# MoBA heads issued in pairs, and the in-projection of block 2 as rounded products of split operands

## What is computed

```
s_own = einsum('bhqd,bhkd->bhqk', q_c, k_own) + bias_own     # masked where key > query
probs = softmax(logits);  out = einsum('bhqk,bhkd->bhqd', p_own, v_own)
```

```
u = h @ w_in
u_q, u_k, u_v, u_cq, u_ckv, u_kr, pool_in = split(u)
```

## Time and profile before

| | us |
|---|---|
| median of 3 runs | 2493.61 |
| lowest and highest run | 2492.33, 2496.37 |
| the profiled execution, own time | 2489.61 |
| its span | 2487.5 |
| PE busy in the span | 2416.9 |
| DVE busy | 1606.2 |
| ACT busy | 1038.0 |

### The profile page before, as it was taken

The page is one execution under the profiler, slowest core; times in us unless marked ns, Lnnn a source line. Parts: engine busy times, 40 slices in busy tenths (PEclk is TensorE's granted clock), DMA queues, the critical chain, the costliest instruction groups (busy, mean ns, idle before and its releaser), DMA issues. The chain is left out here.

```text
span 2487.5 us, 41693 instructions
## 1 busy us (share of the span) xinstructions
PE 2416.9 (97%) x17447; PEld 2057.1 (83%) x17447; DVE 1606.2 (65%) x2242; ACT 1038.0 (42%) x1365; POOL 98.9 (4%) x179
## 2 busy tenths in 40 slices
PE   8999999999999999999999999889999998988999
PEld 7999989999999999899999844454888887647999
DVE  6887756778888887567788533662644443464555
ACT  5445534454454455344544322651422222263333
POOL 2010000001101100000010000000000000000000
PEclk9999999999999999999999999999999999999999
DMA  8776503648777775126477741102433231212452
GB/s 281 252 268 219 162 3 124 208 137 281 251 238 255 268 245 154 34 70 223 146 251 253 281 126 68 35 1 81 156 102 102 86 101 52 85 52 68 158 197 69
DMA packets 270807, 381.97 MB, mean 154 GB/s; under 512 B 9593, under 2 KB 235209, under 8 KB 268994
## 3 DMA queue, kind: packets, MB, share of 16 engines
q1 hardware_dynamic: 251628, 314.47, 38.7%
q0 software_dynamic: 18128, 64.20, 7.2%
q10 hardware_dynamic: 902, 1.15, 0.2%
HBM read 366.13 MB, written 13.65 MB: 153 GB/s over the span
## 5 line engine op out<-in xcount | busy, mean ns | idle before, releaser
L704 PE MATMUL ps<-span 128*128 128x512 f32 x1280 | 453.7, 398 | 1.4 <-issue 1.2
L635 PE MATMUL ps<-span,w_low 128*128 128x256 f32 x1440 | 408.4, 284 | 0.0
L706 PE MATMUL ps<-span,w_low 128*128 128x256 f32 x1280 | 359.4, 281 | 0.0
L633 PE MATMUL ps<-span 128*128 128x256 f32 x1216 | 348.9, 287 | 7.7 <-DVE span L1585 4.7
L1603 DVE TENSOR_TENSOR w_low<-ring,span 128x2048 fp32r<-128x2048 f32 x131 | 299.5, 2286 | 78.1 <-ACT span L1267 78.0
L1267 ACT ACTIVATE span<-ring 128x2048 fp32r<-128x2048 f32 x131 | 250.5, 1914 | 132.3 <-DMA ring<-in_ffn_w_in 110.1
L704 PEld LDWEIGHTS ps<-span 128*128 128x128 f32 x1280 | 240.6, 188 | 59.3 <-issue 1.3
L635 PEld LDWEIGHTS ps<-span,w_low 128*128 128x128 f32 x1440 | 277.2, 192 | 0.0
L634 PE MATMUL ps<-span 128*128 128x256 f32 x864 | 245.6, 284 | 0.0
L633 PEld LDWEIGHTS ps<-span 128*128 128x128 f32 x1216 | 234.1, 193 | 11.8 <-DVE w_low L1603 4.8
L706 PEld LDWEIGHTS ps<-span,w_low 128*128 128x128 f32 x1280 | 241.9, 189 | 0.0
(11 more groups left out here) (487 smaller groups left out, 5340.7 us busy)
## 6 DMA issues: line engine op xcount, KB each, us to landing
ring<-in_ffn_w_in SPq DMA_DIRECT2D x88, 1024.0 KB, 8.9
ring<-in_w_mlp SPq DMA_DIRECT2D x64, 1024.0 KB, 5.3
wmod<-in_w_mod POOLq DMA_DIRECT2D x96, 512.0 KB, 6.8
ring<-in_ffn_w_out SPq DMA_DIRECT2D x44, 1024.0 KB, 5.1
ring<-in_w_mix_in SPq DMA_DIRECT2D x26, 1024.0 KB, 5.6
ring<-in_xattn_w_kv SPq DMA_DIRECT2D x16, 1024.0 KB, 5.5
mod_scratch<-mod_acc POOLq DMA_DIRECT2D x24, 512.0 KB, 6.3
ring<-mod_scratch SPq DMA_DIRECT2D x12, 1024.0 KB, 5.0
```

Source lines behind the costliest of these rows:

```text
L633: mm(dst, w_hi, x_hi, start=start, stop=False, **more)
L635: return mm(dst, w_lo, x_hi, start=False, stop=stop, **more)
L704: mm(ps[bank + m].rearrange("p (w t) -> p w t", w=2), hi[:, k, cols], span[:, :, k, :], start=(k == 0), stop=False, skip_group_check=True)
L706: last = mm(ps[bank + m][:, 0:T], lo[:, k, cols], h_high[:, k, :], start=False, stop=(k == KD - 1), skip_group_check=True)
```

## The change

1. **MoBA in pairs.** PE's order becomes, for p = 0 to 5: scores(pair p), the transposes of both heads of pair p-1, out(pair p-2). Within a pair the bias products come first, then six score products of 128 columns that alternate between the two heads, and four value products that alternate likewise. Waits are taken once for the pair. DVE's and ACT's programs are not changed.
2. **In-projection split.** The input's high half goes to `in_high` (written by ACT's shift), its low half to `h_low`, made by DVE two at a time behind the scales of the next chunk. Each weight tile is rounded by ACT (`in_high_part`) and split by DVE (`in_low_part`), two tiles ahead. All products become `split_mm` with weights stationary; the values now come out by column and are transposed by four PE transposes inside the last tile, which also widens from 32 to 128 columns (its DMA from 128 KB to 512 KB). The order within the first tile becomes chunk by chunk for both halves.
3. **Moved.** The running sums for pooling move from `qm` to `vm`, the pooled result from `vm` to `qm`, since the new buffers lie over `qm`, `km`, `probT` and part of `prob`. The padding memsets move from the pooling stage into the loop over MLA query heads, cut by head. In layer 1 pooling is done for the latent stream alone. The copy of a gain at the start (L3274) goes. In layer 1 the first rounding waits for the wide MLP's last use of `prob` and stands ahead of the squares on ACT.

```diff
-            for h in range(NH + 3):
-                if h < NH:
-                    scores(h)
-                if 2 <= h < NH + 2:
-                    turn(h - 2)
-                if h >= 3:
-                    out(h - 3)
+            for pair in range(NPAIR + 2):
+                if pair < NPAIR:
+                    scores(pair)
+                if 1 <= pair <= NPAIR:
+                    turn(2 * pair - 2)
+                    turn(2 * pair - 1)
+                if pair >= 2:
+                    out(pair - 2)
...
+                early, late = slice(0, P), slice(P, T)
+                for at, q, key in ((0, late, slice(0, P)), (P, late, slice(P, T)), (T, early, slice(0, P))):
+                    for e, bank in enumerate(banks):
+                        hi = slice(e * HD, (e + 1) * HD)
+                        last = mm(bank[:, at:at + key.stop - key.start], mq[hi, pair, q], mk[hi, pair, key],
+                                  start=False, stop=(at == T), skip_group_check=True)
...
+            def out(pair):
+                pe.wait_ge(*pt_ready.at(l, 2 * pair + 2))
+                if pair >= 2:
+                    pe.wait_ge(*av_out.at(l, pair - 1))
+                for k in range(2):
+                    for e in range(2):
+                        h = 2 * pair + e
+                        dst = ps[6 + pair % 2][e * HD:(e + 1) * HD, k * P:T]
+                        last = mm(dst, mv[:, k, h * HD:(h + 1) * HD], probT[:, e, k * T:T + k * P],
+                                  start=(k == 0), stop=(k == 1), skip_group_check=True)
```

```diff
+                pe.wait_ge(*part_low.at(i, n + 1))
                 if n >= 2:
                     pe.wait_ge(*in_evac.at(i, 2 * (n - 1)))
...
+                def product(m, k, c):
+                    ms = slice(m * P, (m + 1) * P)
+                    x_hi = in_high[:, 1, k, :] if c.start else in_high[:, :, k, :]
+                    return split_mm(ps[bank + m][:, c], hi[:, k, ms], lo[:, k, ms], x_hi, h_low[:, k, c],
+                                    k == 0, k == KD - 1)
...
+                if n == 0:
+                    for k in range(KD):
+                        pe.wait_ge(*h_low_ready.at(i, 2 * k + 2))
+                        for m in range(2):
+                            last = product(m, k, ask)
...
+        def in_high_part(i, n):
+            s, use = place(("in", i, IN_TILES[n][0]))
+            act.wait_ge(w_loaded[s].sem, 16 * (use + 1))
+            size = KD * IN_TILES[n][2]
+            go(w_in_high[(n + 1) % 2][:, 0:size], ring[:, s, 0:size], ACT.Copy).then_inc(*part_rounded.up())
...
             else:
+                act.wait_ge(*wide_act.at(0, 3 * KD * WIDE_QUARTERS))
+                in_high_part(i, 0)
                 for q in range(4):
                     for s in (CTX, LAT):
                         square(i, 0, s, q)
...
                 act.wait_ge(w_used[s].sem, use + 1)
+                if n + 2 < len(IN_TILES):
+                    in_high_part(i, n + 2)
...
-            for k in range(KD):
+            in_low_part(i, 0)
+            for k in range(KD + 1):
                 for s in (CTX, LAT):
-                    scale(i, 0, s, k)
+                    if k < KD:
+                        scale(i, 0, s, k)
+                for s in (CTX, LAT):
+                    if k:
+                        low(i, 0, s, k - 1)
+            in_low_part(i, 1)
...
                 roped(slice(0, MQK), ps[2 + u % 2][0:MQK, 0:T], qm[0:MQK, u, cols(LAT)])
+                for padded in (qm, km):
+                    step(i, v.memset(padded[MQK:P, u, :], 0.0), pool_dve)
```

More of the change, by code:

```diff
@@ L786, in moba, with scores @@
         def moba(l):
[L787 to L800, removed]
+            def scores(pair):
+                if pair >= 2:
+                    pe.wait_ge(*sm_act.at(l, 4 * (pair - 1)))
+                banks = [ps[SCORE_BANKS[(2 * pair + e) % 4]] for e in range(2)]
+                for e, bank in enumerate(banks):
+                    h = 2 * pair + e
+                    mm(bank[:, 0:T], cst["flip"], hank[:, h, :], start=True, stop=False,
+                       skip_group_check=True)
+                    mm(bank[:, T:T + P], cst["flip"], hank[:, h, P:T], start=False, stop=False,
+                       skip_group_check=True)
+                early, late = slice(0, P), slice(P, T)
+                for at, q, key in ((0, late, slice(0, P)), (P, late, slice(P, T)), (T, early, slice(0, P))):
+                    for e, bank in enumerate(banks):
+                        hi = slice(e * HD, (e + 1) * HD)
+                        last = mm(bank[:, at:at + key.stop - key.start], mq[hi, pair, q], mk[hi, pair, key],
+                                  start=False, stop=(at == T), skip_group_check=True)
+                        if at == T:
+                            last.then_inc(*sc_done.up())
             def turn(h):
@@ L809, in turn @@
                 last.then_inc(*pt_done.up())
[L811 to L814, removed]
+            def out(pair):
+                pe.wait_ge(*pt_ready.at(l, 2 * pair + 2))
+                if pair >= 2:
                     pe.wait_ge(*av_out.at(l, pair - 1))
[L816 to L820, removed]
+                for k in range(2):
+                    for e in range(2):
+                        h = 2 * pair + e
+                        dst = ps[6 + pair % 2][e * HD:(e + 1) * HD, k * P:T]
+                        last = mm(dst, mv[:, k, h * HD:(h + 1) * HD], probT[:, e, k * T:T + k * P],
+                                  start=(k == 0), stop=(k == 1), skip_group_check=True)
+                        if k:
+                            last.then_inc(*av_done.up())
             pe.wait_ge(*mix_evac.at(l, MIX_TILES - 1))
@@ L2267, in build_second @@
         mod_high = [mod_three[:, j * PIECE:(j + 1) * PIECE] for j in range(3)] + [mod_fourth]
+    with ExitStack() as under:
+        part = lambda name, shape: under.enter_context(nc.sbuf_tensor(name, shape, F32R))
+        part("below_in", [P, BELOW_IN])
+        w_in_high = [part("w_in_high0", [P, SLOT])[:, :]]
+        in_high = part("in_high", [P, 2, KD, T])
+        part("below_prob", [P, BELOW_PROB])
+        w_in_high.append(part("w_in_high1", [P, SLOT])[:, :])
     h_high = [h_both[:, s] for s in range(2)]
@@ L3270, in vector_program @@
         for i in range(DEPTH):
-            v.tensor_copy(key_gain[0:NOPE, i:i + 1], pcol(i, "g_k_mla", rows=NOPE)).then_inc(*key_gain_ready.up())
-        dve.wait_ge(*key_gain_ready.now(0))
-        for i in range(DEPTH):
             ub, ask = unit_base(i), asked(i)
@@ L3287, in vector_program @@
             for m in range(2):
-                for s in range(2):
-                    g = 2 * m + s
-                    step(i, v.tensor_tensor_scan(csum[:, g, first:first + T], ones_row, pin[:, m, cols(s)],
+                for s in streams(i):
+                    step(i, v.tensor_tensor_scan(csum[:, 2 * m + s, first:first + T], ones_row, pin[:, m, cols(s)],
                                                  0.0, ALU.mult, ALU.add), pool_dve)
+            in_low_part(i, 2)
             step(i, v.tensor_copy(csum[:, :, first + T:], csum[:, :, first + T - 1:first + T].to_broadcast(
@@ L3309, in vector_program @@
                                         None, ALU.mult), pool_dve)
-            for padded in (qm, km):
-                step(i, v.memset(padded[MQK:P, :, :], 0.0), pool_dve)
+            in_low_part(i, 4)
             dve.wait_ge(*nrm_act.at(i, NRM_ACT_QK_STD))
```

119 lines of the change are left out of this document (67 added, 52 removed).

## The result

The changed kernel takes 2497.3 us (median of 20 runs, 2493.8 to 2501.1), the kernel before beside it 2493.5 (20 runs). The ratio is 1.0020, 95% interval 1.0013 to 1.0027: slower by 0.2%, where I had forecast 0.3% faster. The changed profiled execution took 2500.4 us (span 2498.3), the one before 2489.6, so the two traces differ by 10.8 us in span, the medians only by 3.8. The traced execution of the kernel before is among its faster ones, that of the changed kernel its third slowest of 20. The table explains the traces. The solver is the part of the mixer that follows MoBA.

What follows compares the result with a forecast made beforehand. PE, busy 97% of the span, was taken to bound the kernel. Terms 0.9 + 11.8 + 3.2 - 3.1 - 1.9 - 2.5 = 8.4 us, off the median 2493.6, gave 2485.2, range 2475 to 2494.

Steps and rivals of the forecast that it cites:

- MoBA's queues: MoBA, both layers: waits for VectorE's weights eat most of 13.8 us PE work saved; gain 0.45 per layer, 0.9 in all.
- the 28 that I had named as a sign of being wrong: MoBA stage: a length under 21 us or over 28 would show the forecast wrong.
- Clock: PE's granted clock: new idles cost 0.5 us in layer 0's in-projection, 1.5 in layer 1's, 0.5 in MoBA; loss 2.5.
- C: Rival, MoBA: idles of 1 to 2 us halve the clock for most of the stage; 17.6 lost, 9 slower, 2503; chance 0.08.
- In-projection, layer 0: Block 2, layer 0: three rounded products replace each plain float32 one; stage ends at 1536.7 against 1548.5, gain 11.8 us.
- In-projection, layer 1: Block 2, layer 1: VectorE paces tile 0 and the rope chain ends last; gain 3.2 us, with 1.5 clock loss counted separately.
- MLA: Layer 1's query-head loop: padding memsets lengthen VectorE's rounds, so rotations wait; loss 3.1 us, 1.4 at 0.44 a memset.
- The wide MLP's end: Layer 0's last wide tiles: a rounding queued on ScalarE ahead of the squares makes PE wait longer; loss 1.9 us.

Runs made afterwards that it cites:

- changed_filled: The changed kernel plus idle 128-column float32 matmuls in PE's MoBA waits, one and four per pair: 2494.4 us, ratio 1.0006 to the kernel before.
- Combined_pool: The changed kernel with VectorE and ScalarE ordered by pairs, weight split later, two in-projection splits moved, padding memsets on GpSimd: 2470.8 us, ratio 0.9916.
- combined_loop: The changed kernel with VectorE and ScalarE ordered by pairs, weight split later, two in-projection splits moved, memsets kept in VectorE's loop: 2475.6 us, ratio 0.9936.
- inproj_pads_pool: The changed kernel with the old MoBA, two in-projection splits moved in their queues and padding memsets on GpSimd: 2477.6 us, ratio 0.9944.
- pairs_alone: The kernel before with only the paired MoBA added, its in-projection unchanged: 2503.1 us, ratio 1.0046.

## Why the prediction was wrong

**MoBA's queues: right in mechanism, about 1 us a layer too kind.** The overlap (0.94 us a pair), the wait in each round and who ends it are in the trace. I gave MoBA itself 24.4 us at full clock, a gain of 0.45 a layer, and said that 13.8 would be eaten by waits. The filled layers without a stretch have 25.3, where the old order has 24.8 (not the 24.6 that I wrote). The 28.5 us of layer 0 in the changed trace also pass the 28 that I had named as a sign of being wrong.

**Clock: the step that failed.** I took 0.5 us for MoBA, a number with no row behind it, against a rival (C) that had the mechanism right. Measured, the two stages lost 9.9 us where my sum without the clock had them gain 0.9: 10.8 apart. Of these 8.8 are the clock (67.8 us for both stages in the changed kernel, against twice 29.5 with fillers and no stretch); the other 2.0 are the queue's, with up to 0.4 of the fillers' own in them. The fillers gave 7.3 of the 8.8 back in changed_filled itself, with one stretch of 3.4 us left. The granted clock averaged 0.985 to 0.988 in the 20 runs of the changed kernel, 0.987 to 0.991 with the fillers, and 0.992 to 0.996 in the runs of the kernel before. Worked out from these averages, with 0.50 and 1.00 as the two levels that the traces show, a run had some 60 to 75 us at half clock with the change and 20 to 40 before (the two traces: 76 and 31); this is an estimate, but it holds for every run and not for one trace. I argued that PE would work more than two thirds of each round, and took that as protection. It worked about 75% (8.96 of 12 us) and was not protected. C was too dear in size (17.6): in layer 0 the stretches covered 9.7 of MoBA's 28.5 us, not most of it, and the rest of them the solver's start, which I had not thought of. The Trainium skill (TensorE: Matmul & The Clock Gate, "HAM oscillation") warned of it; its example is of waits longer than any here, where none was above 2.1 us.

**In-projection, layer 0: right in mechanism, short by a part that is half the clock.** 11.8 predicted; the trace of the change has 8.7 with 10.2 us at half clock in the stage. Combined_pool, with 2.2 us less of a start and only 3.4 us of slow clock, has 12.6. Against combined_loop, whose stage is the same but for 6.8 us more at half clock, it is 1.5 us shorter (82.8 and 84.3), so 1.5 of the 3.1 missing are shown to be the clock.

**In-projection, layer 1: right in mechanism, its clock term too small.** 3.2 less 1.5; the trace has a loss of 0.7, with stretches at 2117.9, 2131.5 and 2162.2. In inproj_pads_pool, where only the one at its start came, the same instructions gain 2.25. The clock term was at least 3 us rather than 1.5.

**MLA: right in mechanism and size.** 3.1 predicted for the memsets, 2.8 measured at full clock; the other 2.2 of the changed trace are again a stretch (2196.4 to 2203.2). The 1.4 that I gave for memsets of 0.44 us does not follow from my own working: six of them stand ahead of the rope that the sixth rotation waits for, so 0.16 less each makes 2.1 of the 3.1. One memset of 512 columns took 0.48 us plus 0.17 of gap. By the one cycle per element of the Trainium skill (VectorE: DVE Perf Modes, "Zero memsets can be issued as uint32 (trn2)") I had estimated 0.53. By the same rule an estimate for 3072 columns is 3.2, where the trace has 2.62, so the measured times lie below the rule.

**The wide MLP's end: right.** 1.9 predicted, 1.8 more of wait measured (5.80 against 4.00), and gone once the rounding stood behind the squares.

The clock term was 2.5 us. Against my steps without the clock the traced stages fell short by some 20 us: 10.8 in MoBA, 3.1 and 3.9 in the in-projections, 2.2 in MLA. Pairs of traces with equal work (but for the fillers in MoBA) show 15.5 of these to be the clock (8.8, 1.5, 3.0 and 2.2), and 2.0 are the queue's in MoBA. Against the 10.9 of gain that I had without the clock, 20 is 9 us of loss, as the stages show. What stays open: the other 2.5 may be the stretches left at the start of both in-projections or errors of size. And the medians differ by 3.8 us only, so the stretches move from run to run, and no trace shows which of them the median run has.

## What to carry to other kernels

Where the matrix engine is 97% busy, work taken off it inside a loop that another engine paces can be no gain but a new wait in every round, and many waits of 1 to 2 us can cost clock on top of their idle time (here 8.8 us on top of the 13.3 that PE waited for the weights). So reorder the queues of the other engines first (all of a pair's work ahead of the next pair's, bulk work where nothing waits behind it), and take matrix work away only then. Price each edit at half clock as well, and look at the granted clock of every stage that the edit makes sparser.

## What the runs showed of the hardware

The clock fell to 0.50 with no wait above 2.1 us, where PE had worked 8.96 of 12 us, and a single wait of 2.3 us in a sparse stage was followed by 10.2 us at 0.50 although PE was busy for 10.0 of them. Idle work in the waits kept the clock up, but for stretches of 3.4 us, and made the kernel faster. A stretch also came where PE had been busy without a gap: in pairs_alone the 14.3 us ahead of 1531.3 were fully busy at 1.00, and the 6.8 us from there (the rest of the eight-row matmuls and the product behind them) were fully busy at 0.50. GpSimd cleared 32 x 3072 float32 elements in 2.65 us, VectorE in 2.62.
